# Two transformer blocks on one core: from barriers and loops to one unrolled section, with the joints between stages done by halves of the tokens

## What is computed

```python
for l in range(2):                                   # first block
    x = x + 0.5 * swiglu_ffn(rms_norm(x), w1, w2)    # 1024 -> 2 x 2816 -> 1024
    h = rms_norm(x)
    y_a, y_b, y_c = gmlp(h @ ..), retention(h @ ..), sparse_attention(h @ ..)
    mix = sum(sigmoid(h @ w_merge_gate_i + b_i) * (y_i @ w_branch_out_i))
    x = x + mix @ w_o
    x = x + 0.5 * swiglu_ffn(rms_norm(x), w1', w2')
x = rms_norm(x, final)
for l in range(2):                                   # second block
    u = rms_norm(x)
    ys = fourier, grouped attention, mLSTM, differential attention of u @ w_in
    x = x + sum(sigmoid(gates_i) * (ys_i @ w_branch_i)) @ w_out
    x = x + (gelu(conv3(a)) * lin) @ w_down          # a, lin = rms_norm(x) @ w_up
out = rms_norm(x, final)
```

## Time and profile before

| | |
|---|---|
| median of 3 runs | 2595.03 us (2592.93 to 2602.33) |
| profiled execution, its time | 2593.43 us |
| its span | 2591.4 us |
| mean granted PE clock | 0.967 |
| busy PE, DVE, ACT, POOL | 94%, 53%, 42%, 15% |
| DMA | 411.8 MB, mean 159 GB/s |

### The profile page before, as it was taken

The page is one execution under the profiler, slowest core; times in us unless marked ns, Lnnn a source line. Parts: engine busy times, 40 slices in busy tenths (PEclk is TensorE's granted clock), DMA queues, the critical chain, the costliest instruction groups (busy, mean ns, idle before and its releaser), DMA issues. The chain is left out here.

```text
span 2591.4 us, 42611 instructions
## 1 busy us (share of the span) xinstructions
PE 2436.8 (94%) x17584; PEld 2291.4 (88%) x17584; DVE 1386.0 (53%) x1544; ACT 1081.7 (42%) x1315; POOL 387.7 (15%) x332
## 2 busy tenths in 40 slices
PE   7998999899989989998997899998998999998997
PEld 6998999899879989988997898988997898988997
DVE  4445555544444455555444535585665544675665
ACT  4334345433343343454333443354443444354443
POOL 1321000022212310000222000000333000000332
PEclk9999999999989998999999999999999999999999
DMA  6554433355345545334553533343543533344553
GB/s 256 185 188 171 184 114 121 124 203 188 136 177 180 187 147 199 125 104 150 200 180 127 190 131 124 123 146 147 201 173 119 188 122 140 118 147 146 187 189 119
DMA packets 61086, 411.79 MB, mean 159 GB/s; under 512 B 7796, under 2 KB 9716, under 8 KB 12952
## 3 DMA queue, kind: packets, MB, share of 16 engines
q1 hardware_dynamic: 60952, 409.89, 44.1%
HBM read 407.24 MB, written 2.10 MB: 158 GB/s over the span
## 5 line engine op out<-in xcount | busy, mean ns | idle before, releaser
L167 DVE TENSOR_TENSOR w_lo<-w_raw,w_hi 128x2048 fp32r<-128x2048 f32 x372 | 861.3, 2319 | 479.2 <-ACT w_hi L163 478.9
L322 PE MATMUL bank<-hT_hi,w_hi 128*128 128x256 f32 x3600 | 1029.8, 286 | 16.0 <-PEq L275 8.1
L324 PE MATMUL bank<-hT_hi,w_lo 128*128 128x256 f32 x3600 | 1021.9, 284 | 0.0
L323 PE MATMUL bank<-hT_lo,w_hi 128*128 128x256 f32 x3600 | 1021.8, 284 | 0.0
L163 ACT ACTIVATE w_hi<-w_raw 128x2048 fp32r<-128x2048 f32 x372 | 709.3, 1907 | 325.4 <-PE bank L324 291.9
L322 PEld LDWEIGHTS bank<-hT_hi,w_hi 128*128 128x128 f32 x3600 | 692.0, 192 | 22.7 <-issue 11.0
L323 PEld LDWEIGHTS bank<-hT_lo,w_hi 128*128 128x128 f32 x3600 | 692.0, 192 | 2.6
L324 PEld LDWEIGHTS bank<-hT_hi,w_lo 128*128 128x128 f32 x3600 | 691.4, 192 | 0.0
L509 POOL TENSOR_TENSOR ffn_g_hi<-ffn_g,ffn_zero 128x256 fp32r<-128x256 f32 x132 | 125.7, 952 | 776.5 <-PE bank L324 704.8
L322 PE MATMUL bank<-w_hi,ffn_g_hi 128*128 128x512 f32 x528 | 209.4, 397 | 13.6 <-POOL ffn_g_lo L511 13.6
L324 PE MATMUL bank<-w_hi,ffn_g_lo 128*128 128x512 f32 x528 | 209.1, 396 | 0.0
(11 more groups left out here) (295 smaller groups left out, 2644.2 us busy)
## 6 DMA issues: line engine op xcount, KB each, us to landing
w_raw<-in_tiles SPq DMA_DIRECT2D x372, 1024.0 KB, 4.8
mid_cmp_w<-in_cmp_w SPq DMA_DIRECT2D x2, 2048.0 KB, 8.2
grow<-in_final SPq DMA_DIRECT2D x4, 512.0 KB, 8.1
bias<-in_bias SPq DMA_DIRECT2D x1, 1536.0 KB
mid_gm_rows<-in_rows SPq DMA_DIRECT2D x2, 768.0 KB, 4.8
rows<-in_rows SPq DMA_DIRECT2D x2, 768.0 KB, 5.5
x_res<-in_x SPq DMA_DIRECT2D x1, 1024.0 KB, 5.0
rel_line<-start_line SPq DMA_DIRECT2D x1, 1024.0 KB, 5.2
```

The costliest lines, as they stand in the source:

```text
L167: eng.tensor_tensor(self.lo[slot][:], self.raw[slot][:], self.hi[slot][:].bitcast(F32), ALU.subtract).then_inc(self.lo_done[slot], 1)
L322: pe.matmul(out, w[0], x[0], start=start, stop=False)
L323: pe.matmul(out, w[0], x[1], start=False, stop=False)
L324: return pe.matmul(out, w[1], x[0], start=False, stop=stop)
```

## The change

- All stages stand in one block, unrolled, with no loop, barrier or stage end. POOL clears the semaphores of the mixers in the course of it. Buffers of the stages lie in one overlay.
- Four slots; the lo part is written over the raw tile, so a load now waits for `used` of the tile before in its slot.
- The joint of two stages goes by token halves. The last two tiles of a stage are done for half 0, then for half 1; the last two down tiles are therefore both held until half 1. The transposes of half 0 of the following norm stand before the last group of half 1. Squares and scaled x are made in pieces of 512 columns. The first two tiles of the next stage are done for half 0, then come the transposes of half 1, then they are done for half 1. In an FFN this makes their matmuls 128 columns wide; in a middle the order of two units is swapped.
- The row norm between the blocks and at the end becomes a part of the joint, by halves too.
- The hi part of g is made by ACT, the lo part by DVE, with two buffers each.
- The last branch has the order (0, 1, 2, 3, 4, 5); one mixer of each block has two more units before its turn.
- The bias tables are smaller, the taps of the convolution are read where they lie, x is loaded by halves, and the bias line is made behind these loads.

```diff
-SLOTS = 3
+SLOTS = 4
-MERGE_ORDER = (0, 1, 4, 2, 3, 5)
+def merge_order(b, branches):
+    return (0, 1, 2, 3, 4, 5) if b == branches - 1 else (0, 1, 4, 2, 3, 5)
...
     def loads_to(self, sp, n):
         for m in range(self.loaded, min(n, len(self.places))):
-            self.k.load(sp, self.stream[self.places[m]], self.slot[m], self.nth[m])
+            slot, at = self.slot[m], self.places[m]
+            if self.before[m]:
+                sp.wait_ge(self.k.used[slot], self.before[m])
+            sp.dma_start(self.k.raw[slot][:], ...).then_inc(self.k.landed[slot], 16)
...
+class Root:
+    def scalar(self, act, t):
+        for n in range(2):
+            act.wait_ge(*self.made(t, n))
+            act.activation(self.sq[:, n], self.k.x[:, t, n * 512:(n + 1) * 512], ACT.Square, ..., accum_out=...)
+    def pool(self, pool, t):
+        pool.wait_ge(k.squared, squared + 1)
+        pool.tensor_scalar(out, ms[:, 0:1], EPS, None, ALU.add).then_inc(k.rooted, 1)
+        pool.wait_ge(k.squared, squared + 2)
+        pool.tensor_tensor(out, out, ms[:, 1:2], ALU.add).then_inc(k.rooted, 1)
+        pool.tensor_tensor(out, out, k.neg_half[:, 0:1], ALU.pow).then_inc(k.rooted, 1)
...
+class Join:
+    def scalar(self, act):
+        self.k.ring.hi_to(act, self.end + 3)
+        for t in range(NT):
+            for root in self.roots:
+                root.scalar(act, t)
+            if self.norm is not None:
+                self.norm.scalar(act, t)
+    def vector(self, dve):
+        for t in range(NT):
+            if self.add is not None:
+                self.add(dve, t)
+            self.k.ring.lo_to(dve, self.end + 2 + t)
+            if self.scale is not None:
+                self.scale.vector(dve, t)
+            if self.norm is not None:
+                self.norm.vector(dve, t)
...
+class Ffn:
+    def tensor(self, pe, following):
+        for t in range(NT):
+            for j in range(2):
+                self.up(pe, 0, j, t)              # 128 tokens
+            if t == 0:
+                self.norm.tensor(pe, 1)
+        for i in range(1, N):
+            for j in range(2):
+                self.up(pe, i, j)
+            if i < N - 1:
+                ... down(i - 1), all tokens
+        for t in range(NT):
+            for i in (N - 2, N - 1):
+                for j in range(2):
+                    if following is not None and t == 1 and i == N - 1 and j == 1:
+                        following.tensor(pe, 0)
+                    last = self.down(pe, i, t, j)
+                if t or i == N - 1:
+                    last.then_inc(used(i), 1)
+    def scalar(self, act):
+        for i in range(FFN_PAIRS):
+            for j in range(2):
+                self.activate(act, i, j)
+                self.k.ring.hi_to(act, self.up_at(i, j) + SLOTS)
+                self.split_hi(act, i, j)
+            if 0 < i < FFN_PAIRS - 1:
+                self.k.ring.hi_to(act, self.up_at(i, 1) + 1 + SLOTS)
+    def vector(self, dve):
+        for i in range(FFN_PAIRS):
+            for j in range(2):
+                self.combine(dve, i, j)
+                if not (last and j):
+                    ring.lo_to(dve, self.up_at(i, j) + SLOTS - 1)
+                self.split_lo(dve, i, j)
+            ring.lo_to(dve, self.up_at(i, 1) + SLOTS - (1 if last else 0))
...
 class Out:                                       # tensor()
+        pe.wait_ge(self.mlo_ok, 2)
+        for t in range(NT):
+            for m in range(2, OUT_TILES):
+                for j in range(2):
+                    if t == j == 1 and m == OUT_TILES - 1:
+                        following.tensor(pe, 0)
+                    last = self.product(pe, m, j, t)
+                if t or m == OUT_TILES - 1:
+                    last.then_inc(used(m), 1)
...
-        f.tensor(pe, 1)
+        f.tensor(pe, 3)
         f.mark("nsa_y")
...
-        f.tensor(pe, 1)
+        f.tensor(pe, 3)
         f.mark("df_y")
```

More of the change, by code:

```diff
@@ L9 @@
 import math
-from contextlib import ExitStack, contextmanager
+from contextlib import ExitStack
 import numpy as np
@@ L111, in __init__ @@
         self.used = [sem(f"w_used{i}") for i in range(SLOTS)]
[L112 to L145, removed]
+        self.res_ok, self.squared, self.rooted, self.xn_dve, self.xn_act, self.turned, self.hT_hi_ok, self.hT_lo_ok = (
+            sem(n) for n in ("x_res_ok", "x_squared", "x_rooted", "xn_dve", "xn_act", "x_turned", "hT_hi_ok",
+                             "hT_lo_ok"))
+        self.sums, self.roots, self.norms, self.convs = 0, 0, 0, 0
     def rsqrt(self, pool, out, mean_square, sem, before):
@@ L152, in rsqrt, with __init__, add, close @@
         pool.tensor_tensor(out, out, self.neg_half[:, 0:n], ALU.pow).then_inc(sem, 1)
[L154 to L168, removed]
-class Ring:
[L182 to L185, removed]
+class Ring:
+    def __init__(self, k, tiles):
+        self.k, self.tiles, self.places, self.signals = k, tiles, [], []
+        self.loaded = self.hi = self.lo = 0
+    def add(self, places, signals):
+        self.places += places
+        self.signals += signals
+        return len(self.places) - len(places)
+    def close(self):
+        self.slot = [n % SLOTS for n in range(len(self.places))]
         self.nth, self.before = [], []
         loads, count = [0] * SLOTS, [0] * SLOTS
-        for n, s in enumerate(signals + [0, 0]):
-            j = self.slot[n]
-            loads[j] += n >= 2
+        for j, s in zip(self.slot, self.signals):
+            loads[j] += 1
             self.nth.append(loads[j])
@@ new lines, with __init__, vector @@
+class RowScale:
+    def __init__(self, k, root, grow, grow_in, beside):
+        self.k, self.root, self.grow, self.grow_in = k, root, grow, grow_in
+        self.sum = Sum(k, beside)
+    def vector(self, dve, t):
+        self.root.ready(dve, t)
+        dve.wait_ge(*self.grow_in)
+        for n in range(2):
+            xs = self.k.x[:, t, n * 512:(n + 1) * 512]
+            dve.scalar_tensor_tensor(out=xs, in0=xs, scalar=self.root.out[:, t:t + 1],
+                                     in1=self.grow[:, n * 512:(n + 1) * 512], op0=ALU.mult, op1=ALU.mult
+                                     ).then_inc(self.k.res_ok, 1)
@@ L705, in product @@
             make = features_major if role[0] in ("T", "half") else tokens_major
-            last = make(pe, k, slot, half, out)
+            ready = (lambda c: self.norm.ready(pe, half, c)) if n == self.n0 else None
+            last = make(pe, k, slot, half, out, ready=ready)
             if last_half:
@@ new lines, in sync, with scalar, vector @@
+    def sync(self, sp, waits):
+        for wait in waits:
+            sp.wait_ge(*wait)
+        self.k.ring.loads_to(sp, self.end + 1)
+    def scalar(self, act):
+        self.gqa.squares(act)
+        self.fourier.scalar(act)
+        self.gqa.scalar(act)
+        self.mlstm.scalar(act)
+        self.diff.scalar(act)
+        self.out.scalar(act)
+    def vector(self, dve):
+        self.gqa.rope(dve)
+        self.fourier.vector(dve)
+        self.gqa.vector(dve)
+        self.mlstm.vector(dve)
+        self.diff.vector(dve)
+        self.out.vector(dve)
```

1265 lines of the change are left out of this document (629 added, 636 removed).

## The result

| | before | changed kernel |
|---|---|---|
| median, beside each other on one chip | 2594.72 us (2592.93 to 2602.33) | 2645.94 us (2642.49 to 2650.27) |
| profiled execution, its time | 2593.43 us | 2642.49 us |
| its span | 2591.4 us | 2640.8 us |
| mean granted PE clock | 0.967 | 0.972 |

The ratio is 1.0193 [1.0166, 1.0219]: the changed kernel is 51 us slower, and the forecast said 2643. The sum was right, its terms were not: the start came out 24 us dearer than its term, nearly all the others came out cheaper than theirs, and the two cancelled.

A forecast was written before the change was run, and what follows sets the result against it. PE bounds the kernel, busy 94%. Joint, narrow-matmul, start, end and middle terms (5.6 - 0.4 + 1.5 + 54.8 + 8.4 + 1.6 - 1.6 - 21) sum to +48.9 us on 2593.4, giving 2643; range 2587 to 2785, about 0.8.

The forecast's parts named there:

- What waits last at the joints: New joints: squares of half 0 wait for ScalarE's hi split of tile end+2; PE waits 9.7 us before the transposes.
- the first rival: Joints: squares don't wait for tile end+2, PE waits 2.5 us and not 9.7; 65 us less, 2578; chance 0.13.
- The price of narrow matmuls: First two FFN tiles: 192 matmuls of 128 columns at 0.111 us replace 96 at 0.12; +9.8 us per FFN.
- The estimate after the Trainium skill: Narrow FFN matmuls: about 81 ns each, +4.0 us per FFN, the sum about 35 us less; the forecast did not adopt it.
- The start: Start to the first FFN: narrow matmuls and transposes end at 38.4 where today's end at 36.8; +1.6 us.
- The upper bound of part two: Narrow FFN matmuls at 0.22 us, as plain fp32 or if the clock stays at half: 42 us, +31 per FFN.
- the second rival: Six FFNs: narrow matmuls cost double, by fp32 price or half clock; 126 us more, 2769; chance 0.20.
- The middles: Inside the middles: reordered units remove 15.8 us of waits and about 5 us of half clock; -21 us.
- The waits for w lo (8.7) and four_m stay: Inside the middles: PE's waits for w lo, 8.7 us, and for four_m were to remain.
- The rival of the four slots that starve PE: Behind the 2 MB load and the tables: waits of 5 to 10 us at four places, 2665; chance 0.07.
- The w_lo wait at the end of an FFN: FFN end: splits take 5.6 us against 2.74 us of PE work; 2.9 us wait, about 4 with the convolution.
- The smaller joints and the end: FFN to middle +5.6 (block one), -0.4 (block two); between blocks +1.5; FFN to FFN +8.4; end -1.6 us.

The follow-up runs named there:

- e1: Changed kernel with ScalarE's hi split of weight tile end+2 moved from before the squares to after the norm at all joints; 2571.12 us, ratio 0.9902.
- e3: Changed kernel with two extra unread fp32 matmuls of 512 columns after the transposes of half 0, at the start only; 2625.87 us, ratio 1.0114.
- e9: e6 without its two extra fp32 matmuls at the start; 2505.43 us, with e6 beside it at 2497.01.
- e10: e6 with VectorE's lo split of a weight tile put behind the norm of each half at every joint; 2521.75 us, ratio 0.9702.
- e4: Changed kernel with the reordering in the middles undone (last branch's unit order, units before the last mixer's turn); 2668.00 us, ratio 1.0274.
- e8: Changed kernel with only VectorE's lo split moved before the last g; 2624.26 us, ratio 1.0110.
- e6: Changed kernel with hi split after the norm, lo split before last g, two extra matmuls at the start, only first FFN tile in halves; 2496.49 us.

## Why the prediction was right, and where it was not

**What waits last at the joints: right.** The prediction named ScalarE's split of tile end+2, whose load hangs on a signal 2.74 us after half 0, as the thing before the squares. The timeline shows it to 0.1 us at the start and the end of the split, and e1 shows that it decides: its removal gives 75 us, where the first rival ("the joints are short") had put 65. That rival's time was 2578; with the edit that makes it true the kernel takes 2571. The wait itself was over-sized, 9.7 for 8.1, in the last links: the squares overlap with the read of the accumulator, and the last two GpSimd operations were taken at about 0.8 each from the earlier trace rows and took 0.19 and 0.57.

**The price of narrow matmuls: right at five FFNs.** 0.112 against 0.111. The estimate after the Trainium skill (TensorE: Matmul & The Clock Gate, Back-to-back issue gap), 0.081, does not hold for these 4-byte weights.

**The start: this step failed.** "But then 21.3 + 1.3 us of narrow matmuls and transposes end at 38.4, ... +1.6" took the full clock for granted. The upper bound of part two said what would happen if the clock stays at half, and the second rival named it for all six FFNs or none. It came true at one, for 20 of the 25.4 us. The runs showed 192 matmuls 0.213 apart in place of 0.111, and 23 wide ones behind them at the same spacing; the first stood at 17.24, 1.4 us later than forecast. e3 and e9 show that the clock is the cause at the start, and in e10 the same level comes at five joints.

**The middles: right mechanism for the order, term too small.** -21 was 15.8 of waits and 5 of half clock; the four middles lost 30.7, of which the order of units is 22 to 24 (e4). "The waits for w lo (8.7) and four_m stay" was wrong for w_lo: two waits of 3.3 us are gone, and with them most of the 6.6 us beyond. The rival of the four slots that starve PE has nothing for it: the longest wait for w_lo left in a middle is 1.05 us, where it had 5 to 10 at four places.

**The w_lo wait at the end of an FFN: right.** 2.9 forecast and about 4 with the convolution; measured 2.44 at four places, and 4.14 and 2.95 at the two with the convolution. e8 shows what it is worth, 20 us with what follows it.

**The smaller joints and the end** came out 1 to 2.5 us better each than forecast, mostly by the shorter wait. The +0.8 us of four steady FFNs (153.09 to 153.90) and the -0.8 us of the other two are open.

The start cost 24 us more than forecast; the middles came out 10 us lower, the joints 13 and the end 2.5. The forecast of 2643 for 2646 owes its closeness to that, and this was luck. Two slips in the sum are small: 13.0 and a scaled x of 0.5 to 0.7 make 13.5 to 13.7 and not 13.8, and 2595.0 + 48.9 is 2643.9, not 2643.

## What to carry to other kernels

When a normalization is split in halves so that one half hides the other, look at what each in-order queue has in front of the first operation of the chain: here one weight split of 1.9 us, waiting for its load, cost 75 us of 2646, and the fix was to issue it one step later. Cover costs matmuls: give the hidden chain as much as it is long (one tile in halves), not more. And where narrow matmuls follow a gap, carry both prices, 0.112 and 0.213 us, until a trace shows which one holds: here the first held at five FFNs and the second at one.

## What the runs showed of the hardware

- 128-column matmuls in this 4-byte format start 0.112 us apart at 2.4 GHz and 0.213 at 1.2 GHz; 256 columns take 0.12 and 0.213. So halving a tile raises its price from 0.120 to 0.224 us for each wide matmul at 2.4 GHz, and from 0.213 to 0.426 at 1.2 GHz.
- Once PE was at the lower level, it stayed there through stretches of narrow matmuls of 43 us (changed kernel) and 22 us (e9), with eight transposes in the middle, and of 10 us (e10); among the wide ones behind them it rose. Once, in e8, it rose at the transposes between narrow ones, so an execution can go either way.
- A wait of 1.3 us before the transposes was followed by the lower level at five joints of e10, waits of 0.64 to 0.68 at the same joints of e6 were not, and a wait of 2.89 in e1 was not either.
- From 17 to 65 us of the changed kernel the granted clock reads 1.00 while the matmuls are spaced as at 0.5; later, at the joint of e10, it reads 0.52. At the very start of an execution the spacing has to be read, not the clock.
- A one-column GpSimd operation takes 0.19 to 0.22 us alone (the power 0.57) and 1.7 to 2.1 us when it meets VectorE's split of two SBUF tensors (2.3 us long), ending within 0.1 us of that.
